# Routed experts in three reduced-precision products of split parts, with two scatter sums

## What is computed

```
def swiglu(x, w1, w3, w2):
    return (jax.nn.silu(x @ w1) * (x @ w3)) @ w2
...
def run_block(args):               # 128 slots of one expert
    xb, e = args
    return swiglu(xb, w_e1[e], w_e3[e], w_e2[e])
...
return jax.ops.segment_sum(yd * wd[:, None], td, num_segments=t)
```

## Time and profile before

| | |
|---|---|
| three runs | 1903.95, 1907.87, 1909.98 us; median 1907.87 |
| the profiled execution | 1919.32 us; its span, first to last instruction, 1917.5 us |
| granted TensorE clock, mean over the span | 0.963 |
| busy: PE, PEld, DVE, ACT, POOL | 1776.2, 1082.7, 574.9, 375.2, 429.7 us |
| transfers | 346.37 MB, mean 181 GB/s; in the stage of the routed experts 333 GB/s |
| routed experts, first transposes to last down product | 1080.7 to 1885.9 us of the span |

### The profile page before, as it was taken

One profiled execution on the slowest core, in us unless ns is written; L12 is line 12 of the kernel. 1 busy time (PEld: TensorE's weight loads), 2 busy tenths in 40 slices (PEclk: granted clock), 3 DMA queues, 4 the chain that ended last, 5 costly groups with the idle time before them and its releaser, 6 DMA issues. The chain is left out here.

```text
span 1917.5 us, 21807 instructions
## 1 busy us (share of the span) xinstructions
PE 1776.2 (93%) x7487; PEld 1082.7 (56%) x7487; DVE 574.9 (30%) x1221; ACT 375.2 (20%) x722; POOL 429.7 (22%) x630
## 2 busy tenths in 40 slices
PE   7979999869999799999987699999999999999993
PEld 2457767456666599996553344444444444444441
DVE  2344454354455500211562021111211111211213
ACT  3112222122223412210210111111111111111110
POOL 0010000020010333321007123332233332233221
PEclk9989999989999899999988799999999999999996
DMA  9411212200000332235241499999999999999852
GB/s 328 141 45 44 87 45 86 78 22 1 0 0 0 110 77 76 67 88 171 93 184 59 170 333 340 349 340 324 326 340 338 336 325 324 328 331 324 295 186 112
DMA packets 127327, 346.37 MB, mean 181 GB/s; under 512 B 20698, under 2 KB 60206, under 8 KB 109240
## 3 DMA queue, kind: packets, MB, share of 16 engines
q1 hardware_dynamic: 105130, 301.18, 43.0%
q0 software_dynamic: 21440, 42.08, 9.3%
q10 hardware_dynamic: 720, 2.62, 0.3%
HBM read 332.01 MB, written 45.25 MB: 197 GB/s over the span
## 5 line engine op out<-in xcount | busy, mean ns | idle before, releaser
L1825 PE MATMUL psum<-mem 128*128 128x512 f32 x1120 | 495.4, 595 | 1.1 <-DVE mem L1870 1.1
L1825 PEld LDWEIGHTS psum<-mem 128*128 128x128 f32 x1120 | 208.4, 191 | 237.9 <-issue 236.2
L1810 PE MATMUL psum<-mem 128*128 128x512 f32 x560 | 252.0, 593 | 1.4 <-DVE mem L1882 1.4
L1886 DVE TENSOR_TENSOR mem<-mem,psum 128x256 f32<-128x256 f32 x70 | 29.5, 421 | 439.8 <-ACT mem L1857 439.8
L1810 PEld LDWEIGHTS psum<-mem 128*128 128x128 f32 x560 | 101.0, 190 | 102.5 <-issue 102.5
L1754 POOL TENSOR_TENSOR held<-nhalf 1x1 f32<-1x1 f32 x207 | 37.9, 183 | 476.8 <-DMA sums<-mem,si 399.4
L1781 POOL DMA_INDIRECT sums<-mem,si x70 | 112.2, 1603 | 38.4 <-issue 38.4
L1877 DVE TENSOR_SCALAR mem<-psum,mem 128x512 f32<-128x512 f32 x70 | 52.6, 751 | 206.6 <-PE psum L1810 120.7
L1857 ACT ACTIVATE mem<-psum 128x256 f32<-128x256 f32 x70 | 26.9, 384 | 440.0 <-PE psum L1825 440.0
L653 PE MATMUL psum<-mem 128*128 (+2 forms) x288 | 99.9, 447 | 9.3 <-ACT mem L764 7.1
L764 ACT ACTIVATE mem<-psum,small 128x640 f32<-128x640 f32 (+1 forms) x80 | 56.7, 709 | 242.9 <-DVE small L863 242.7
(11 more groups left out here) (249 smaller groups left out, 2527.0 us busy)
## 6 DMA issues: line engine op xcount, KB each, us to landing
mem<-in_w_e SPq DMA_DIRECT2D x210, 1024.0 KB, 12.5
mem<-in_w_mod SPq DMA_DIRECT2D x8, 2048.0 KB, 7.9
mem<-in_w_mod SPq DMA_DIRECT2D x8, 1024.0 KB, 12.2
mem<-in_x_sample SPq DMA_DIRECT2D x8, 512.0 KB, 11.2
mem<-in_w_in SPq DMA_DIRECT2D x1, 4096.0 KB, 14.4
wkvb<-in_w_in SPq DMA_DIRECT2D x8, 512.0 KB, 4.4
mem<-in_w_in SPq DMA_DIRECT2D x8, 512.0 KB, 4.3
mem<-in_w_out SPq DMA_DIRECT2D x1, 4096.0 KB, 16.7
```

The costliest lines, as they stand in the source:

```text
L1810: mm = pe.matmul(pY[:, c * 512:(c + 1) * 512], gT[:, f, :], w2[v][:, f, c * 512:(c + 1) * 512], start=(f == 0), stop=(f == 1))
L1825: mm = pe.matmul(pH.rearrange("p (a n) -> p a n", a=2), xT[:, k, :], w13[u][:, :, k, :], start=(k == 0), stop=(k == KT - 1))
```

## The change

- Up and down products of the routed experts become three fp32r products each (`thrice`). ACT makes all hi parts (`xHi`, `wHi13`, `gHi`, `wHi2`), DVE the lo parts, except the second half of `wLo2`, which POOL makes (`lo_w2`). `wLo13` and `wLo2` are written over the raw weights in the ring.
- The split of `w13` is made one block ahead (`next_w13`, for block n+1 in step n). ACT takes the whole of `take_y`.
- The ACT order in a step is: `take_x(n)`, `next_w13(n+1)`, `take_y(n-2)`, `take_g(n-1)`, `hi_w2(n)`, `silu(n)`. The DVE order: `take_x(n)`, `next_w13(n+1)`, `take_g(n-1)`, `lo_w2(n)`, `product(n)`. The POOL order: `gather(n)`, `lo_w2(n-2)`, `scatter(n-3)`.
- Even blocks scatter into `sums`, odd ones into `sums1`, each with a semaphore, an index tile and a `yb` of its own, so a scatter waits for the one two before. `sums1` is zeroed from `xg[1]` before, and the last block loads both and adds them.
- `w2` is read so that a partition gets one run of 8 KB in place of two of 4 KB, and the product is written in matching order.
- Eight steps instead of four stand in front of the loop; one barrier with a clearing of 18 semaphores is added after the mixer stage.

```
+    nc.clear_and_free_semaphores(list(sk.values()) + list(sg.values()))
+    nc.all_engine_barrier()
...
-    w2_src = I["w_e2"][0].rearrange("e (f p) n -> p e f n", p=P)
+    w2_src = I["w_e2"][0].rearrange("e (p f) n -> p e f n", p=P)
...
+            sp.wait_ge(s_zero, 1)
+            for t in range(NT):
+                sp.dma_start(S["sums1"][t * P:(t + 1) * P, :], xg[1]).then_inc(s_acc0, 16)
...
         # gpsimd
+                def lo_w2():
+                    v = (u - 2) % RING
+                    pool.wait_ge(se["h2"], n - 1)
+                    pool.tensor_tensor(wLo2[v][:, 1, :], w2[v][:, 1, :], wHi2[v % 2][:, 1, :].bitcast(F32),
+                                       ALU.subtract).then_inc(se["l2P"], 1)
                 def scatter():
-                    m = n - 3
-                    if not (first and u == 3):
-                        pool.wait_ge(s_sc, 16 * m)
+                    m, b = n - 3, (u - 3) % 2
+                    if not (first and m < 2):
+                        pool.wait_ge(s_sc[b], 32 * i + 16 * ((u - 3) // 2))
                         hold(pool, 1)
...
-                    pool.wait_ge(se["yV"], m + 1)
-                    pool.wait_ge(se["yA"], m + 1)
+                    pool.wait_ge(se["ye"], m + 1)
                     hold(pool)
...
         # tensor
+            def thrice(out, xh, xl, wh, wl, first, last):
+                pe.matmul(out, xh, wh, start=first, stop=False)
+                pe.matmul(out, xl, wh, start=False, stop=False)
+                return pe.matmul(out, xh, wl, start=False, stop=last)
...
                 def up():
-                    pe.wait_ge(se["xeV"], n + 1)
-                    pe.wait_ge(se["xeA"], n + 1)
-                    pe.wait_ge(s_w13[u], 32 * (i + 1))
+                    pe.wait_ge(se["xl"], 2 * n + 2)
+                    pe.wait_ge(se["l13"], 2 * n + 2)
                     for k in range(KT):
-                        mm = pe.matmul(pH.rearrange("p (a n) -> p a n", a=2), xT[:, k, :], w13[u][:, :, k, :],
-                                       start=(k == 0), stop=(k == KT - 1))
+                        mm = thrice(pH.rearrange("p (a n) -> p a n", a=2), xHi[:, k, :], xLo[:, k, :],
+                                    wHi13[u % 2][:, :, k, :], wLo13[u][:, :, k, :], k == 0, k == KT - 1)
...
         # scalar
+            def hi_w13(n, i, u):
+                act.wait_ge(s_w13[u], 32 * (i + 1))
+                for a in range(2):
+                    act.activation(wHi13[u % 2][:, a], w13[u][:, a], ACT.Copy).then_inc(se["h13"], 1)
...
+                def next_w13():
+                    if not (isinstance(n, int) and n == 0):
+                        act.wait_ge(se["u"], n)
+                    hi_w13(n + 1, i + (u + 1) // RING, (u + 1) % RING)
...
+                    act.activation(yb[u % 2], pY, ACT.Copy, scale=wslot(tabs, m, 2).bitcast(F32)).then_inc(se["ye"], 1)
...
+                def hi_w2():
+                    act.wait_ge(s_w2[u], 16 * (i + 1))
+                    if not (isinstance(n, int) and n < 2):
+                        act.wait_ge(se["y"], n - 1)
+                    act.activation(wHi2[u % 2][:, :, :], w2[u], ACT.Copy).then_inc(se["h2"], 1)
...
+            act.wait_ge(s_acc, 16 * NT)
+            hi_w13(0, 0, 0)
             run(act, step)
...
         # vector
+            def lo_w13(n, u):
+                for a in range(2):
+                    dve.wait_ge(se["h13"], 2 * n + a + 1)
+                    dve.tensor_tensor(wLo13[u][:, a], w13[u][:, a], wHi13[u % 2][:, a].bitcast(F32), ALU.subtract)\
+                       .then_inc(se["l13"], 1)
...
+                def lo_w2():
+                    dve.wait_ge(se["h2"], n + 1)
+                    dve.tensor_tensor(wLo2[u][:, 0, :], w2[u][:, 0, :], wHi2[u % 2][:, 0, :].bitcast(F32),
+                                      ALU.subtract).then_inc(se["l2V"], 1)
...
         # last block, sync and vector
+                sp.dma_start(yt1[:, t, :], sums[1][t * P:(t + 1) * P, :]).then_inc(s_yt[t], 16)
...
+                dve.tensor_tensor(r, r, yt1[:, t, :], ALU.add).then_inc(s_cb, 1)
```

More of the change, by code:

```diff
@@ L1676, in _ @@
             dve.wait_ge(s_k8, 2 * NT)
-            for b in range(2):
-                dve.memset(xg[b], 0.0).then_inc(se["z"], 1)
+            dve.memset(xg[0], 0.0).then_inc(se["z"], 1)
             dve.wait_ge(s_er, 1)
@@ L1685, in build, with run @@
     with nc.Block() as block:
-        def run(eng, step, total=None):
-            for u in range(RING):
-                step(u, 0, u, lambda k, u=u: None if u >= k else False)
-            with eng.Fori(1, NE // RING) as i:
+        LAST = NE // RING - 1
+        def run(eng, step):
+            for n in range(2 * RING):
+                step(n, n // RING, n % RING, lambda k, n=n: None if n >= k else False)
+            with eng.Fori(2, LAST) as i:
                 for u in range(RING):
@@ L1759, in gather @@
                 def gather():
-                    if first and u < 2:
+                    if first and n < 2:
                         return
@@ L1987 @@
         "sums": nc.dram_tensor("sums", [TOK, D], F32, kind="Internal").ap(),
+        "sums1": nc.dram_tensor("sums1", [TOK, D], F32, kind="Internal").ap(),
     }
```

118 lines of the change are left out of this document (75 added, 43 removed).

## The result

| | changed kernel | kernel before, same chip |
|---|---|---|
| median of 4 runs each | 1938.76 us (1930.65 to 1943.32) | 1907.78 us |
| ratio | 1.0159, interval 1.0137 to 1.0180 | |
| profiled execution | 1930.65 us, span 1928.8 | 1919.32 us, span 1917.5 |
| mean step, X(1) to X(69), 68 steps | 11.56 us | 11.36 us |

It is slower by 31 us, where 1896 was forecast. The profiled execution of the changed kernel is the fastest of its four, 8.1 us under their median; spread over 69 steps that is 0.12 us a step, so steps of two profiled executions that differ by 0.1 us can't be told apart.

What follows compares the result with a forecast made beforehand. PE was taken as the bound, with DMA and a loop through POOL next. 69 x (11.1 - 11.36) - 4.8 + 3.4 - 1.4 + 7 + 1.5 = -12 from 1907.9 gave 1896 us; own range 1889 to 1902, overall 1851 to 1955.

Steps and rivals of the forecast that it cites:

- the POOL loop: Expert stage: `take_y`, `held`, scatter, next gather and its landing span two steps; 10.45 us a step unblocked, 11.24 if `held` waits.
- (b): POOL blocked once by DVE and that loop alone binding: 11.24 us a step, 1906 us; 19% with steps up to 11.36.
- (a): POOL blocked twice, `lo_w2` holding back DVE's `xLo`, then `held` waiting: 12.0 us a step, 1958 us; 25%, in full or part.
- the blend: Forecast step of 11.1 us, from DMA at 11.0 and POOL's loop at 10.45 to 11.24; 38% for 11.0 to 11.18.
- The issue at X + 12.2: On POOL: gather issued 12.2 us after X, the start of `turn_x(n)`, if `held` waits until DVE's subtractions are through.
- The landing: The gather's time from issue on POOL until its rows have landed, carried over from the kernel before as 10.3 us.
- The transfers at 11.0: DMA engines in the expert stage: weight loads mixed with gathers and scatters cost a fixed 11.0 us a block.
- the three at 9.5: Start of the expert stage: first three steps run at about 9.5 us from weights already there, -4.8 us.
- Drain: End of the expert stage: two shorter down products, about 9.9 us in place of 11.3 to the last scatter, -1.4 us.
- the point of decision: On POOL: a gather issued later than X + 12.4 decides for the case of POOL blocked twice.
- (d): PE's clock falling because PE idles 2 us a step; near 17 us a step if all products slow; 8% with other delays.
- the share of 0.93 with a gather issued later than X + 12: Sign in the profile after: DMA share fallen to 0.93, with `held` or the gather's issue this late, means POOL's loop binds.

Runs made afterwards that it cites:

- e5: Changed kernel plus two unused float32 products of 512 columns on PE ahead of each step's transposes; 1938.8 us, ratio 1.0152 to the kernel before.
- b1: Kernel before with the two scatter sums alone, products still fp32; 1921.4 us, ratio 1.0036 to the kernel before.
- e4: Changed kernel, but each scatter waits until the one before it has landed, as with a single sum; 1995.5 us, ratio 1.0412 to the kernel before.
- e16: Changed kernel with about half of the routed rows neither gathered nor scattered, that part of the result left out; 1934.2 us, ratio 1.0129.
- e3: Changed kernel with `take_y` ahead of `next_w13` in ACT's order; 1909.9 us, ratio 0.9970 to the kernel before.
- e11: Changed kernel with `take_y` and `take_g` before `next_w13`, gather first on POOL, low part of `w2` whole on DVE; 1911.1 us, ratio 0.9973.
- e14: Changed kernel with `take_y` and `take_g` ahead of `next_w13`, low part of `w2` whole on DVE, gather still behind the scatter; 1906.7 us, ratio 0.9991.
- e1b: Changed kernel with POOL issuing the next gather ahead of `lo_w2` and the scatter; 1904.5 us, ratio 0.9980 to the kernel before.
- e8: Changed kernel with `take_y` and `take_g` ahead of `next_w13` and the gather first on POOL; 1937.9 us, ratio 1.0106 to the kernel before.
- e15: Changed kernel with `take_y` first on ACT, gather first on POOL, low part of `w2` whole on DVE; 1895.2 us, ratio 0.9930.

## Why the prediction was wrong

**The step that failed** is "The step I take: DMA at 11.0 and the POOL loop between 10.45 and 11.24; two limits so near each other rarely both hold exactly, so 11.1." Both ends of that range for the POOL loop were wrong. The lower end needs a POOL that isn't held up, and in the changed kernel it was held up in 40 of 40 steps. The upper end allows one hold-up for each gather, and in 15 of the 40 there were two: 25.2 us for two steps, or 12.6 a step, where the other 25 took 22.5, or 11.24. The mean is 23.5 us for two steps, 11.7 a step, above the DMA's 11.0. When two limits lie near each other the larger one holds, or more than it if it doesn't run smoothly. The text had both cases before it: one hold-up was in (b)'s 19%, shared with other cases, two were in (a)'s 25%, and the blend under both got 38%.

**What it cost.** The forecast gave the 69 steps 69 x 11.1 - 4.8 = 761.1 us; they took 795.3. Of these 34 us, 2.5 lie in the first three steps (31.0 in place of 28.5), 9 are the 0.14 us between 11.1 and 11.24 over the other 66, and 22 are the mean of 11.58 above 11.24. The 34 us are most of the 43 between 1896 and 1939. Of the rest, 8.1 + 1.8 are the distances of the two profiled executions from their medians (above); the ends cancel to within a microsecond.

**What was right by luck.** The issue at X + 12.2 came out at 12.27, but as the mean of two kinds of step: 11.64 with one hold-up, 13.31 with two. The 22.5 us of (b) came out to the tenth in the steps with one hold-up, as 11.64 + 10.85, where the forecast had 12.2 + 10.3. The scatter follows `held` by 0.17 us and not by 0.54, so the issue came earlier. The landing, carried over as 10.3 us, has a median of 11.1, and of 11.7 in e5.

**The separate parts.** Products of 512 columns stand 0.233 us apart (forecast 0.226). ACT's 2048 columns take 1.92 (1.94), `take_y` 1.11 (1.14), DVE's 2048 columns 2.29 (2.33), 512 0.69 (0.67), 256 0.42 (0.39), POOL's half 2.42 (2.41). DVE's product behind SiLU takes 0.60 where 0.39 was taken. Every engine had room, as said; the weights never came late, as said.

**The two sums** were rightly put at nothing in the loop (b1: 11.36 both) and +7 in the last block (+7.6, b1 6.3). That a single sum would bind beside the late `take_y` is e4.

**The transfers at 11.0.** As the bound of this kernel it was wrong; e16 takes a tenth of the share away and the time stays. As a size it was somewhat high. The same product of share and step, 11.0 us in the kernel before, is 0.980 x 11.00 = 10.8 in e3 and 0.951 x 11.10 = 10.6 in e11, so the price of the mix isn't fixed. Part of the difference may be the longer runs of `w2`, which the forecast counted as 0 of a possible 0.5; no run tries them alone.

**The ends.** First step +2.5 (forecast +3.4). First steps: 8.74 and 10.5, then 11.8; the three at 9.5 were not there, since the chain is in force from the third on. Drain +0.2 (-1.4): its last down products start at the full clock and fall to the low one from 1887.8 us on, 0.43 us apart. Expert block starts +0.4 later (+1.5 for the barrier).

**The rivals.** (b) and (a) both happened, in turns. Rival (a) put the gather's issue at X + 13.7 and the step at 12.0; the 15 steps held up twice have 13.31 in the mean, and 12.6 us. It wasn't DVE's `xLo` that POOL's `lo_w2` held back, as (a) had it, but the pair behind it (5.73 us in the timeline above). 14 of the 40 gathers were issued later than X + 12.4, the point of decision, and 22 in e16. (d): the forecast expected nothing of a short pause, and the granted clock was 0.94 over the stage, 0.50 for at least 5 us behind the pause of 3.04 us. What that costs stays open, since e5 pays for the clock with PE time. Of the signs that were named ahead, the share of 0.93 with a gather issued later than X + 12 was the one for the POOL loop, and "POOL's small operations wait more than once a step" the one for a forecast that fails. The profile shows both.

**Left open:** what holds e14 and e1b; what the low clock costs without a filler; why the gather lands sooner in e3; whether one hold-up in every step, without the second, would give 11.24 us, since e5, which has just that, pays for its filler; whether a `held` made by an operation that reads nothing would run unblocked beside DVE, which wasn't tried; and how much lower the step could go with fewer bytes.

## What to carry to other kernels

When the pacing engine is relieved, list every loop that crosses engines and queues, with its length over its number of buffers, and take the longest, not a mean. Then ask of each hold-up in it whether it can happen twice in some steps: here a short step was always followed by one with two. A small operation on GpSimd that stands before a DMA issue costs whatever VectorE subtraction it falls under (1.45 to 2.26 us in place of 0.18), so the place of a two-input VectorE operation is part of the price of moving work. Splitting weights belongs behind the eviction that releases the next scatter and gather: reordering two calls on ACT (e3) was worth as much as the whole change lost.

## What was not expected of the hardware

- `held`, one element on GpSimd: 0.18 us alone, 1.45 to 2.26 beside a two-input VectorE subtraction in the timelines above, 0.18 beside a VectorE zeroing of the same 2048 columns.
- The hold-up goes both ways: a VectorE subtraction of 2.28 us took up to 5.25 us, a GpSimd one of 2.42 up to 3.50 (e8).
- Half of the rows less, at the same number of indirect transfers, shortened the gather's landing only from 11.1 to 10.0 us. With all rows it was 8.5 us in e15, where the last scatter had been issued 8 us before, and 11.1 and 11.7 in the changed kernel and e5, where that was 2.8 and 2.6 us. Other things differ between these kernels, so this isn't shown to be the cause.
- fp32r products of 512 columns stand 0.233 us apart at a granted clock of 1.00 and 0.43 at 0.50. After 3.04 us of idle time the clock was found at 0.50 in the changed kernel. After 1.91 us in its drain the products began 0.23 us apart and fell to 0.43 after 1.5 us. In e5 the clock was 1.00 from 1200 to 1700 us.
